# Latent products in high and low parts, latents split behind their norm, rotary keys copied behind the queries

## The chip, the core and the metric

The kernel runs on one core of one Trainium2 chip. TensorE (PE) does the matrix products, VectorE (DVE) and ScalarE (ACT) the work on whole tiles, GpSimd (POOL) one subtraction per weight slot and a few gathers, SyncE (SP) issues the weight transfers. The metric is the device time of one execution in microseconds (us), the median of several runs.

## What is computed

512 tokens of width 1024 pass through a first block (RG-LRU, sparse attention over latents, a routed mixture of experts) and then through two equal layers (neighbourhood, differential and latent attention, a gated feed-forward). All is in float32. The parts that the change touches are the products that read a normalised latent. In the first block:

```python
c_kv = rmsnorm(ckv, kv_norm_g)                       # (512, 256)
k = einsum('sr,rhd->shd', c_kv, w_uk)                # 8 heads of 128
v = einsum('sr,rhd->shd', c_kv, w_uv)
```

The reference folds `w_uk` into the queries and `w_uv` into the outputs; the kernel forms keys and values, which is the same sum. In each of the two layers:

```python
q  = rms_norm(c_q, q_norm_g) @ w_qb                  # 384 -> 8 heads of 64 + 32 rotary
kv = rms_norm(c_kv, kv_norm_g) @ w_kvb               # 256 -> 8 heads of 64 keys + 64 values
k  = concat([k_nope, broadcast(rope(k_rope))])       # one rotary key for all heads
o  = blocked_attention(q, k, v, 96 ** -0.5)
```

## The kernel before

Activations stand transposed, 128 features on the partitions and all 512 tokens in a row, so a product is one 128x128 weight chunk against 128x512 columns (for values the latent is the 128x128 side and the weight has the columns). The weights stream in slots of 16 chunks (1 MB) through a ring of five, `wring`. SP loads a slot when the one five places before is used up, and `w_used` counts slots that PE has left: it rises with PE's first matmul on the next slot.

There are two kinds of product. `tile` does one plain float32 matmul for each chunk, which the profile shows as two records. `tile3` does three matmuls in fp32r for each chunk: high weight by high operand, high weight by low operand, low weight by high operand (L459 to L461). For these, slots are split: `weights_hi` on ACT (L508) copies a slot into one of three `w_hi` buffers, and waits for `w_used` of the slot that held the buffer before; `weights_lo` on POOL (L518) then subtracts, and writes the low part over the ring's slot (`w_lo`, 128x2048). PE waits for `lo_rdy` of a split slot, and for the transfer alone of one that isn't split. Before the change the slots of uk and uv (28 and 29 of the first block) and of qb, kvb_k and kvb_v (29 to 31 of each layer) are not split.

The order of each engine is written out by hand; semaphores connect them. Around the change in a layer:

- **PE** runs the list `MIXED`: output tiles o0 to o7 of the differential attention, between them gate tiles ml_g0 to ml_g2, the squares of the latents (`squares_pe`, L470, behind `sq_added`) and the spreading of their norms (`spread_pe`, L479). For the second latent, ckv2, this reads o4, ml_g2, squares, o5, o6, spread, o7. Then come the rotary key's turn (L1120), the six query tiles of qb on `cq` with two turns between (L1056), four key tiles of kvb_k and four value tiles of kvb_v (L1137) on `ckv2`, and then the attention (L802), behind `roped` and `keys_rdy`. Tiles go to a small set of PSUM banks; from the third on, a tile needs the bank that ACT's copy of two tiles before has freed.
- **DVE** spreads the norm (L590), scales the latent in place (L1426, `lat_rdy`), merges output tiles (L1333, L1338), adds up squares (L564, L566), rotates the shared key (L1429 to L1432, `kr_rdy`), copies it to all heads (`k96`, L1435, `keys_rdy`), and rotates the queries in two groups (L1439, L1440, four additions L1444 each, `roped`).
- **ACT** applies the gates (L1183), copies the raw queries behind `kr_rdy` (`raw`, L1178), converts two slots (L508), copies queries (L1289, L1290), keys, and, behind `roped`, the values `vM` (L1178). In the attention it converts a further slot at units 4, 19 and 33 (`ml_weights`).
- **POOL** goes through the split slots in order.

In the first block uk and uv (L448, L2474) follow the queries, DVE scales `ckv` at L1984 long before, and the top-k selection runs on DVE beside them.

Of the kernel before, what the change touches and what calls it, by code (L numbers as in the profile page):

```python
# [8 lines left out]
P = 128  # L9
# [160 lines left out]
def build(nc, xT, wmod, wrest, wfirst, wlayers, consts, vectors, brow, frow, lamv, rpb, w13, w2, out):  # L170
# [2 lines left out]
    vcol, NVEC = vector_plan()  # L173
    n_slots1, n_slots2 = end1 // CHUNKS, size2 // CHUNKS

    unsplit = [("rg", "ckv"), ("uk", "att_out")]
    plain1 = {s for a, b in unsplit for s in range(one[a] // CHUNKS, one[b] // CHUNKS)} | {one["router"] // CHUNKS}
    plain2 = set(range(two["qb"] // CHUNKS, two["ml_g"] // CHUNKS))
    split = [s for s in range(n_slots1) if s not in plain1]
    split += [n_slots1 + l * n_slots2 + s for l in range(LAYERS) for s in range(n_slots2) if s not in plain2]  # L180
    order = {slot: q for q, slot in enumerate(split)}

    def split_no(slot):
# [3 lines left out]
    with ExitStack() as ctx:  # L187

        def at(name, kb, shape, dt=F32):
            return nc.alloc_sbuf_tensor_at(name, shape, dt, offset=(nc.sbuf_base + 2047) // 2048 * 2048 + int(kb * 1024))  # L190
# [251 lines left out]
        def tile(pe, bank, c0, rhs, nk, m=P, wait=None):  # L442

            for k in range(nk):
                w = chunk(pe, c0 + k)
                if wait is not None:
                    wait(k)
                ins = pe.matmul(bank, w[:, 0:m], rhs[:, k, :], start=(k == 0), stop=(k == nk - 1))  # L448
                if k < nk - 1:
                    said(ins)  # L450
            return ins

        def tile3(pe, bank, c0, hi, lo, nk, m=P, wait=None):

            for k in range(nk):
                wh, wl = chunk(pe, c0 + k)
                if wait is not None:
                    wait(k)
                said(pe.matmul(bank, wh[:, 0:m], hi[:, k, :], start=(k == 0), stop=False))  # L459
                pe.matmul(bank, wh[:, 0:m], lo[:, k, :], start=False, stop=False)  # L460
                ins = pe.matmul(bank, wl[:, 0:m], hi[:, k, :], start=False, stop=(k == nk - 1))  # L461
            return ins

        def squares_pe(pe, n):

# [129 lines left out]
            spread(dve)  # L595

        rstd = acc[:]

        def free_bank_b(dve):

# [411 lines left out]
        def layer_pe(pe, l):  # L1012
# [106 lines left out]
            pe.wait_ge(A.free, kr_copied)  # L1119
            pe.matmul(B.claim(pe)[0:MLA_QK, :], K("perm_m")[0:MLA_QK, 0:MLA_QK], krT[0:MLA_QK, :], start=True, stop=True).then_inc(B.full, 1)  # L1120

            pe.wait_ge(lat_rdy, (l + 1) * (MQC + KVC))
            turns = []
            for t in range(QB_TILES):
                tile(pe, A.claim(pe), base["qb"] + t * MQC, cq, MQC).then_inc(A.full, 1)
                if t < HEADS // 4:
                    turns.append(A.made)
                else:
                    n = t - HEADS // 4
                    if n < len(turns):  # L1130
                        turn(K("perm_m"), turns[n])
            for h in range(0, HEADS, 2):
                tile(pe, A.claim(pe), base["kvb_k"] + (h // 2) * KVC, ckv2, KVC).then_inc(A.full, 1)
            for s_ in range(NQB):
                b = A.claim(pe)
                for k in range(KVC):
                    ins = pe.matmul(b, ckv2[:, k, s_ * P:(s_ + 1) * P], chunk(pe, base["kvb_v"] + 4 * k, 4), start=(k == 0), stop=(k == KVC - 1))  # L1137
                    if k < KVC - 1:
                        said(ins)
                ins.then_inc(A.full, 1)  # L1140
# [35 lines left out]
        def layer_act(act, l):  # L1176
# [114 lines left out]
            for h in range(0, HEADS, 2):  # L1291
                two_heads(q96, h)
                if h == 0:
                    weights_hi(act, base["kvb_k"])
            act.wait_ge(merged_rdy, (3 * l + 2) * DC)
            for h in range(0, HEADS, 2):
                two_heads(k96, h)
# [27 lines left out]
        def layer_dve(dve, l):  # L1325
# [89 lines left out]
            for n, parts in enumerate(MIXED):  # L1415
                for kind, m in parts:
                    if kind == "o":
                        merge(1, m)
                if n in (1, 3):
                    sum_squares(dve, (MQC, KVC)[n // 2])  # L1420
                    inverse_root(dve, (MQ_RANK, KV_RANK)[n // 2], EPS)
                elif n in (2, 4):
                    X, c_n, g = ((cq, MQC, V(f"mq_g{l}")), (ckv2, KVC, V(f"mkv_g{l}")))[n // 4]
                    spread(dve)
                    for c in range(c_n):
                        STT(out=X[:, c, :], in0=X[:, c, :], scalar=g[:, c:c + 1], in1=rstd, op0=ALU.mult, op1=ALU.mult).then_inc(lat_rdy, 1)  # L1426
# [4 lines left out]
            dve.wait_ge(B.free, B.took)  # L1431
            TT(x, x, t, ALU.add).then_inc(kr_rdy, 1)  # L1432
            dve.wait_ge(kr_rdy, l + 1)

            dve.tensor_copy(k96[64:MLA_QK, :, :], krT[64:MLA_QK, :].unsqueeze(1).broadcast_to((32, HEADS, SEQ))).then_inc(keys_rdy, 1)  # L1435
            for g in range(HEADS // 4):
                x, t = raw[:, g, :], vM[:, g, :]
                dve.wait_ge(A.free, a + g + 1)
                step(TT(t, x, K("cos_m"), ALU.mult))  # L1439
                TT(x, B.take(dve), K("sin_m"), ALU.mult).then_inc(B.free, 1)  # L1440
                dve.wait_ge(B.free, B.took)
                for j in range(4):
# [233 lines left out]
        def _(act):  # L1676
# [184 lines left out]
        def _(dve):  # L1861
# [112 lines left out]
            for n in range(MOD_SLOTS):  # L1974
                dve.wait_ge(rest_mod_in[n % 2], 16 * (n // 2 + 1))
                for h in range(2):
                    ins = mod_tile(mods[:, n % 2, h * D:(h + 1) * D], MOD_FIRST + 2 * n + h)
                ins.then_inc(mod_used, 1)
                if n == 0:
                    inverse_root(dve, KV_RANK, EPS)  # L1980
                if n == 1:
                    spread(dve)
                    for c in range(KVC):
                        dve.scalar_tensor_tensor(out=ckv[:, c, :], in0=ckv[:, c, :], scalar=V("kv_g")[:, c:c + 1], in1=rstd,  # L1984
                                                 op0=ALU.mult, op1=ALU.mult).then_inc(ckv_rdy, 1)
                score_in(2 * n)
                score_in(2 * n + 1)
            dve.wait_ge(mod_used, 1 + MOD_SLOTS)
# [403 lines left out]
        def _(pe):  # L2392
# [71 lines left out]
                tile3(pe, A.claim(pe), one["q"] + m * DC, *u, DC).then_inc(A.full, 1)  # L2464
            pe.wait_ge(ckv_rdy, KVC)
            for m in range(HEADS):
                tile(pe, A.claim(pe), one["uk"] + m * KVC, ckv, KVC).then_inc(A.full, 1)
            for s in range(NQB):
                for n in range(2):
                    b = A.claim(pe)  # L2470
                    for k in range(KVC):

                        w = chunk(pe, one["uv"] + (2 * k + n) * 4, 4)
                        ins = pe.matmul(b, ckv[:, k, s * P:(s + 1) * P], w, start=(k == 0), stop=(k == KVC - 1))  # L2474
                        if k < KVC - 1:
                            said(ins)
                    ins.then_inc(A.full, 1)
            pe.wait_ge(gh_rdy, RC)
            rnn_bank = {}

# [467 lines left out]
```

## Time and profile before

| | us |
|---|---|
| median of 3 runs | 3163.84 |
| lowest, highest run | 3163.22, 3166.88 |
| span of the profiled execution | 3164.0 |
| PE busy | 3055.2 |
| DVE busy | 1653.4 |
| ACT busy | 992.4 |
| POOL busy | 974.6 |

The profiled execution's span, first to last instruction, is 3164.0 us, and its own time can be taken as that. In the profile, a busy PE is one with a matmul in its pipe; a record's length includes the pipe (0.39 us for a matmul that is followed by the next one after 0.23 us), so rates are read from starts. The timeline gives start, length, engine, line, output and inputs, a count for equal instructions in a row, and in brackets the idle time just before with what ended it. PEclk is the share of TensorE's full clock that was granted.

### The profile page before, as it was taken

Reading aid. Unit: us, or ns where it says so; the run is one execution under the profiler, and the core shown is the slowest. Engines: PE = TensorE matmul, PEld = TensorE weight load, DVE = VectorE, ACT = ScalarE, POOL = GpSimd, SP = SyncE. Lnnn points to the kernel's source line nnn. Section 1 sums busy time; section 2 is a strip of 40 time slices with the busy share of each in tenths; the row PEclk is TensorE's granted clock in tenths of the full one; section 3 lists DMA queues with packets and bytes.
Section 4 is the critical chain, followed back from the end, with each engine's and each line's share of the span. In section 5 each row is a group of like instructions: output and inputs, shape, how many; then the busy total and the mean of one; then the engine's idle time right before and its main releaser. Section 6 shows DMA issues by size and latency. Waiting matters only on the chain.

```text
span 3164.0 us, 34626 instructions
## 1 busy us (share of the span) xinstructions
PE 3055.2 (97%) x13776; PEld 2108.2 (67%) x13776; DVE 1653.4 (52%) x2794; ACT 992.4 (31%) x1415; POOL 974.6 (31%) x423
## 2 busy tenths in 40 slices
PE   7999999999999989999999999999999999999998
PEld 4777656743333367776656788887786765778886
DVE  5698956455554535574657422221757457732223
ACT  3653233200000144334343322223424444332212
POOL 3243103210000044332213544446442311444433
PEclk9999999999999999999999999999999999999999
DMA  6236212599999921211211222222121120222221
GB/s 258 95 112 247 107 54 85 208 384 427 427 427 427 414 79 67 79 68 54 93 41 67 80 93 94 106 94 90 64 81 66 67 93 14 92 81 93 94 94 53
DMA packets 64817, 448.44 MB, mean 142 GB/s; under 512 B 8526, under 2 KB 8814, under 8 KB 12448
## 3 DMA queue, kind: packets, MB, share of 16 engines
q1 hardware_dynamic: 60336, 436.25, 35.8%
q0 software_dynamic: 3760, 8.11, 0.8%
q8 instruction: 98, 1.61, 0.2%
q10 hardware_dynamic: 576, 2.10, 0.2%
q14 instruction: 47, 0.39, 0.0%
HBM read 445.93 MB, written 4.21 MB: 142 GB/s over the span
## 4 chain that ended last, share of the span: by engine, by line
PE 82%; DVE 8%; DMA 7%; ACT 2%; issue 1%; SPq 0%; DVEq 0%; ACTq 0%
PE ps L459 16%; PE ps L460 15%; PE ps L461 15%; DMA mring<-w 6%; PE ps L2576 3%; PE ps L802 2%; PE ps L781 2%; PE ps L2640 2%; PE ps L2488 2%; PE ps L448 2%; PE ps L783 2%; PE ps L782 2%; PE ps L972 2%; PE ps L1076 1%; PE ps L2577 1%
## 5 line engine op out<-in xcount | busy, mean ns | idle before, releaser
L518 POOL TENSOR_TENSOR w_lo<-wring,w_hi 128x2048 fp32r<-128x2048 f32 (+1 forms) x284 | 854.6, 3027 | 1636.5 <-ACT w_hi L508 1636.4
L459 PE MATMUL ps<-x_hi,w_hi 128*128 128x512 f32 (+1 forms) x1480 | 582.2, 393 | 8.5 <-ACT lru_t L1729 4.5
L461 PE MATMUL ps<-x_hi,w_lo 128*128 128x512 f32 (+1 forms) x1480 | 577.1, 390 | 0.0
L508 ACT ACTIVATE w_hi<-wring 128x2048 fp32r<-128x2048 f32 x176 | 335.9, 1911 | 317.8 <-PE ps L459 242.4
L460 PE MATMUL ps<-xf_lo,w_hi 128*128 128x512 f32 x1080 | 421.3, 390 | 0.0
L459 PEld LDWEIGHTS ps<-x_hi,w_hi 128*128 128x128 f32 (+1 forms) x1480 | 278.0, 188 | 77.7 <-ACT gb L1753 5.2
L461 PEld LDWEIGHTS ps<-x_hi,w_lo 128*128 128x128 f32 (+1 forms) x1480 | 278.1, 188 | 59.1
L2576 PE MATMUL ps<-mring,xT__96 128*64 128x512 f32 x512 | 238.2, 601 | 12.5 <-DMA mring<-w 7.2
L2577 PE MATMUL ps<-mring,xT__96 128*64 128x512 f32 x512 | 238.2, 601 | 0.0
L460 PEld LDWEIGHTS ps<-xf_lo,w_hi 128*128 128x128 f32 x1080 | 203.5, 188 | 41.2
L1457 DVE TENSOR_TENSOR g_f<-ps,g_f 128x512 f32<-128x512 f32 x44 | 30.4, 692 | 362.8 <-PE ps L461 350.0
L781 PE MATMUL ps<-x_hi,w_hi 128*128 128x512 f32 x336 | 162.3, 483 | 0.0
L460 PE MATMUL ps<-xa_lo,w_hi 128*128 128x512 f32 (+1 forms) x400 | 155.7, 389 | 0.0
L459 PE MATMUL ps<-g_hi,w_hi 128*128 128x512 f32 x352 | 137.7, 391 | 0.0
L461 PE MATMUL ps<-g_hi,w_lo 128*128 128x512 f32 x352 | 137.0, 389 | 0.0
L460 PE MATMUL ps<-g_lo,w_hi 128*128 128x512 f32 x352 | 137.0, 389 | 0.0
L1315 ACT ACTIVATE g_f<-ps 128x512 f32<-128x512 f32 x44 | 26.3, 598 | 351.4 <-PE ps L461 346.5
L1584 POOL DMA_INDIRECT xs<-u_rows,ids x15 | 15.4, 1029 | 391.4 <-PE ps L2563 365.1
L2576 PEld LDWEIGHTS ps<-mring,xT__96 128*64 128x64 f32 x512 | 65.1, 137 | 101.8 <-issue 82.3
L783 PE MATMUL ps<-x_hi,w_lo 128*128 128x512 f32 x336 | 132.1, 393 | 0.0
L782 PE MATMUL ps<-xa_lo,w_hi 128*128 128x512 f32 x336 | 131.9, 393 | 0.0
L2640 PE MATMUL ps<-mring,hidT 128*64 128x512 f32 x512 | 117.8, 597 | 2.6 <-DMA mring<-w 1.6
(567 smaller groups left out, 5563.5 us busy)
## 6 DMA issues: line engine op xcount, KB each, us to landing
mring<-w SPq DMA_DIRECT2D x192, 1024.0 KB, 23.2
wring<-wlayers SPq DMA_DIRECT2D x148, 1024.0 KB, 4.7
wring<-wfirst SPq DMA_DIRECT2D x44, 1024.0 KB, 4.8
mods<-wrest SPq DMA_DIRECT2D x16, 1024.0 KB, 4.8
wmodS<-wmod SPq DMA_DIRECT2D x3, 2048.0 KB, 17.6
rp<-rpb POOLq DMA_DIRECT2D x16, 192.0 KB, 2.7
hT<-xT SPq DMA_DIRECT2D x1, 2048.0 KB, 8.8
wmodS<-wmod SPq DMA_DIRECT2D x2, 1024.0 KB, 26.4
```

What stands on the lines that cost most here:

```text
L448: ins = pe.matmul(bank, w[:, 0:m], rhs[:, k, :], start=(k == 0), stop=(k == nk - 1))
L459: said(pe.matmul(bank, wh[:, 0:m], hi[:, k, :], start=(k == 0), stop=False))
L460: pe.matmul(bank, wh[:, 0:m], lo[:, k, :], start=False, stop=False)
L461: ins = pe.matmul(bank, wl[:, 0:m], hi[:, k, :], start=False, stop=(k == nk - 1))
L508: act.activation(w_hi[:, q % HI_SLOTS, :], wring[:, home(g), :], ACT.Copy).then_inc(hi_rdy, 1)
L518: ins = pool.tensor_tensor(w_lo[:, home(slot), o:o + n], wring[:, home(slot), o:o + n], w_hi[:, q % HI_SLOTS, o:o + n].bitcast(F32), ALU.s ...
L781: said(pe.matmul(state["bank"], wh, x[0][:, k, :], start=(k == 0), stop=False))
L782: pe.matmul(state["bank"], wh, x[1][:, k, :], start=False, stop=False)
L783: ins = pe.matmul(state["bank"], wl, x[0][:, k, :], start=False, stop=(k == DC - 1))
L2576: pe.matmul(ps[MOE_ROWS:P, 2 + a, :], x, w[:, 0:SEQ], start=(k == 0), stop=(k == DC - 1))
L2577: ins = pe.matmul(ps[0:MOE_ROWS, 2 + a, :], x, w[:, SEQ:D], start=(k == 0), stop=(k == DC - 1))
L2640: ins = pe.matmul(ps[n * MOE_ROWS:(n + 1) * MOE_ROWS, 5 + a, :], hidT[:, a, k, :], w[:, n * SEQ:(n + 1) * SEQ], start=(k == 0), stop=(k == 3))
```

## The change

The slots of uk, uv, qb, kvb_k and kvb_v are now split, and their products go through `tile3` (weights first) or the new `latent_values` (latent first). `latent_split` takes the place of the scaling in place: DVE writes the scaled latent to a scratch tile, casts it to a high part, and subtracts to get the low part, each step for all chunks before the next, with a wait between. PE waits for the first latent alone ahead of qb, and for the second ahead of kvb_k. The copy of the rotary key to all heads stands behind the rotation of the queries, since its place now holds scratch. ACT converts two more slots in the first block and three more in each layer, POOL subtracts as many.

```diff
-    unsplit = [("rg", "ckv"), ("uk", "att_out")]
+    unsplit = [("rg", "ckv"), ("rnn_out", "att_out")]
...
-    plain2 = set(range(two["qb"] // CHUNKS, two["ml_g"] // CHUNKS))
...
+        def latent_values(pe, s, at, hi):
+
+            b = A.claim(pe)
+            for k, c in enumerate(at):
+                wh, wl = chunk(pe, c, 4)
+                xh, xl = (x[:, k, s * P:(s + 1) * P] for x in (hi, ckv_lo))
+                said(pe.matmul(b, xh, wh, start=(k == 0), stop=False))
+                pe.matmul(b, xh, wl, start=False, stop=False)
+                ins = pe.matmul(b, xl, wh, start=False, stop=(k == KVC - 1))
+            ins.then_inc(A.full, 1)
...
+        def latent_split(dve, X, y, hi, lo, n, g, rdy):
+
+            for c in range(n):
+                ins = dve.scalar_tensor_tensor(out=y[:, c, :], in0=X[:, c, :], scalar=g[:, c:c + 1], in1=rstd, op0=ALU.mult, op1=ALU.mult)
+            after(dve, ins, dve_step, "dstep")
+            for c in range(n):
+                ins = dve.tensor_copy(hi[:, c, :], y[:, c, :])
+            after(dve, ins, dve_step, "dstep")
+            for c in range(n):
+                dve.tensor_tensor(lo[:, c, :], y[:, c, :], hi[:, c, :].bitcast(F32), ALU.subtract).then_inc(rdy, 1)
...
-            pe.wait_ge(lat_rdy, (l + 1) * (MQC + KVC))
+            pe.wait_ge(lat_rdy, l * (MQC + KVC) + MQC)
             turns = []
             for t in range(QB_TILES):
-                tile(pe, A.claim(pe), base["qb"] + t * MQC, cq, MQC).then_inc(A.full, 1)
+                tile3(pe, A.claim(pe), base["qb"] + t * MQC, cq_hi, cq_lo, MQC).then_inc(A.full, 1)
...
+            pe.wait_ge(lat_rdy, (l + 1) * (MQC + KVC))
             for h in range(0, HEADS, 2):
-                tile(pe, A.claim(pe), base["kvb_k"] + (h // 2) * KVC, ckv2, KVC).then_inc(A.full, 1)
+                tile3(pe, A.claim(pe), base["kvb_k"] + (h // 2) * KVC, ckv2_hi, ckv_lo, KVC).then_inc(A.full, 1)
             for s_ in range(NQB):
...
+                latent_values(pe, s_, [base["kvb_v"] + 4 * k for k in range(KVC)], ckv2_hi)
...
                 if h == 0:
-                    weights_hi(act, base["kvb_k"])
+                    weights_hi(act, base["kvb_k"], 1)
+            weights_hi(act, base["kvb_k"])
...
-            dve.tensor_copy(k96[64:MLA_QK, :, :], krT[64:MLA_QK, :].unsqueeze(1).broadcast_to((32, HEADS, SEQ))).then_inc(keys_rdy, 1)
             for g in range(HEADS // 4):
...
+            dve.wait_ge(A.free, a + QB_TILES)
+            dve.tensor_copy(k96[64:MLA_QK, :, :], krT[64:MLA_QK, :].unsqueeze(1).broadcast_to((32, HEADS, SEQ))).then_inc(keys_rdy, 1)
...
             for h in range(HEADS):
                 act.activation(kT[:, h, :], A.take(act), ACT.Copy).then_inc(A.free, 1)
+                if h == 0:
+                    weights_hi(act, one["uk"], 1)
```

`weights_hi` converts all split slots up to a few ahead of the one it is called for, so where slots become split, conversions move although the calls stay. The following lists give an engine's instructions in the order of the program; line numbers are those of the kernel listed.

DVE in layer 0, from the spread of the norm of cq to the sum of the squares of ckv2 (`acc`; `sqb` are squares from ACT), before:

```order
L590 COPY acc<-ps 128x512
L1426 SCALAR_TENSOR_TENSOR cq<-cq,vec,acc 128x512 x3
L1333 SCALAR_TENSOR_TENSOR df_gate<-df_gate,ps 128x512
L1338 TENSOR_TENSOR uT<-uT,df_gate 128x512
L564 COPY acc<-sqb 128x512
L566 TENSOR_TENSOR acc<-acc,sqb 128x512
```

and after:

```order
L603 COPY acc<-ps 128x512
L615 SCALAR_TENSOR_TENSOR cq_y<-cq,vec,acc 128x512 x3
L618 CAST cq_hi<-cq_y 128x512 x3
L621 TENSOR_TENSOR cq_lo<-cq_y,cq_hi 128x512 x3
L1354 SCALAR_TENSOR_TENSOR df_gate<-df_gate,ps 128x512
L1359 TENSOR_TENSOR uT<-uT,df_gate 128x512
L577 COPY acc<-sqb 128x512
L579 TENSOR_TENSOR acc<-acc,sqb 128x512
```

The three scalings write to scratch, and three casts and three subtractions stand between them and the merge of o4.

DVE in layer 0, from the rotation of the shared key `krT` to the first row of the attention, before:

```order
L1429 TENSOR_TENSOR raw<-ps,cs 32x512
L1430 TENSOR_TENSOR krT<-krT,cs 32x512
L1432 TENSOR_TENSOR krT<-krT,raw 32x512
L1435 COPY k_135<-krT 32x4096
L1439 TENSOR_TENSOR vM<-raw,cs 128x512
L1440 TENSOR_TENSOR raw<-ps,cs 128x512
L1444 TENSOR_TENSOR q_134<-vM,raw 32x512 x4
L1439 TENSOR_TENSOR vM<-raw,cs 128x512
L1440 TENSOR_TENSOR raw<-ps,cs 128x512
L1444 TENSOR_TENSOR q_134<-vM,raw 32x512 x4
L867 TENSOR_REDUCE small<-ps 128x1
```

and after:

```order
L1451 TENSOR_TENSOR raw<-ps,cs 32x512
L1452 TENSOR_TENSOR krT<-krT,cs 32x512
L1454 TENSOR_TENSOR krT<-krT,raw 32x512
L1459 TENSOR_TENSOR vM<-raw,cs 128x512
L1460 TENSOR_TENSOR raw<-ps,cs 128x512
L1464 TENSOR_TENSOR q_141<-vM,raw 32x512 x4
L1459 TENSOR_TENSOR vM<-raw,cs 128x512
L1460 TENSOR_TENSOR raw<-ps,cs 128x512
L1464 TENSOR_TENSOR q_141<-vM,raw 32x512 x4
L1466 COPY k_142<-krT 32x4096
L891 TENSOR_REDUCE small<-ps 128x1
```

The copy of the key (`k`) moved from ahead of the queries' rotation to behind it.

ACT in layer 0, from the squares of ckv2 to the first copies of keys, before:

```order
L494 ACTIVATE sqb<-ckv_131 128x512 x2
L1183 ACT_TABLE_LOAD
L1183 ACTIVATE sg_123<-ps,small 128x512
L553 ACT_TABLE_LOAD
L553 ACTIVATE small<-small 128x4
L1178 ACTIVATE raw<-ps 128x512 x2
L508 ACTIVATE w_hi<-wring 128x2048
L1289 ACTIVATE q_134<-ps 64x512
L1290 ACTIVATE q_134<-ps 64x512
```

and after:

```order
L507 ACTIVATE sqb<-ckv_131 128x512 x2
L521 ACTIVATE w_hi<-wring 128x2048
L1203 ACT_TABLE_LOAD
L1203 ACTIVATE sg_123<-ps,small 128x512
L566 ACT_TABLE_LOAD
L566 ACTIVATE small<-small 128x4
L1198 ACTIVATE raw<-ps 128x512 x2
L521 ACTIVATE w_hi<-wring 128x2048
L1309 ACTIVATE q_141<-ps 64x512
L1310 ACTIVATE q_141<-ps 64x512
```

One conversion now stands ahead of the gate ml_g2, and one more behind the copies of the queries, ahead of those of the keys. In the attention, the conversion at unit 4 is two in a row (L521 `w_hi<-wring 128x2048 x2`), where it was one.

## Rows read from the trace of the kernel before

**Rows 1.** the page, the chain that ended last, shares of the span by engine.

```profile
PE 82%; DVE 8%; DMA 7%; ACT 2%; issue 1%; SPq 0%; DVEq 0%; ACTq 0%
```

**Rows 2.** PE's timeline, layer 0: start, length (us), engine, line, operation, [idle, releaser].

```profile
1537.70 0.50 PE L459 MATMUL ps<-o_hi,w_hi 128*128 128x512 f32 x1
...
1546.00 0.95 PE L470 MATMUL ps<-cs,acc 128*128 128x1 f32 x8
...
1557.05 7.89 PE L448 MATMUL ps<-cq,wring 128*128 128x512 f32 x18
...
1581.09 7.03 PE L1137 MATMUL ps<-wring,ckv 128*128 128x512 f32 x16
1589.01 1.10 PE L802 MATMUL ps<-k,q 96*128 96x512 f32 x2 [0.89 <-ACT vM L1178]
...
1604.88 0.64 PE L972 MATMUL ps<-PT,cs 128*64 128x512 f32 x1 [1.19 <-ACT PT L917]
```

**Rows 3.** DVE's timeline, layer 0.

```profile
1539.01 2.08 DVE L1426 SCALAR_TENSOR_TENSOR cq<-cq,vec,acc 128x512 f32<-128x512 f32 x3
...
1542.78 0.69 DVE L566 TENSOR_TENSOR acc<-acc,sqb 128x512 f32<-128x512 f32 x1
...
1559.88 2.29 DVE L1435 COPY k<-krT 32x4096 f32<-32x4096 f32 x1
...
1566.63 9.67 DVE L1444 TENSOR_TENSOR q<-vM,raw 32x512 f32<-32x512 f32 x4
...
1577.78 2.83 DVE L1444 TENSOR_TENSOR q<-vM,raw 32x512 f32<-32x512 f32 x4
```

**Rows 4.** ACT's timeline, layer 0.

```profile
1546.20 0.69 ACT L1183 ACTIVATE sg<-ps,small 128x512 f32<-128x512 f32 x1 [11.08 <-PE ps L461]
...
1559.89 0.60 ACT L1178 ACTIVATE raw<-ps 128x512 f32<-128x512 f32 x1 [11.48 <-DVE krT L1432]
...
1562.90 1.90 ACT L508 ACTIVATE w_hi<-wring 128x2048 fp32r<-128x2048 f32 x1
```

**Rows 5.** PE's timeline, the first block's queries, keys and values.

```profile
365.69 0.39 PE L459 MATMUL ps<-x_hi,w_hi 128*128 128x512 f32 x1
...
366.37 0.39 PE L459 MATMUL ps<-x_hi,w_hi 128*128 128x512 f32 x1
...
373.85 13.89 PE L448 MATMUL ps<-ckv,wring 128*128 128x512 f32 x32
387.58 1.88 PE L2474 MATMUL ps<-wring,ckv 128*128 128x512 f32 x4
```

**Rows 6.** DVE's timeline, start of the first block's attention.

```profile
402.83 0.29 DVE L992 SCALAR_TENSOR_TENSOR Bb<-cs,sel 128x128 f32<-128x128 f32 x1 [11.22 <-PE ps L802]
```

**Rows 7.** DVE's timeline, layer 0: split, merge, later an FFN split.

```profile
1509.57 0.43 DVE L1353 CAST o_hi<-o 128x512 fp32r<-128x512 f32 x1
...
1510.63 0.42 DVE L1353 CAST o_hi<-o 128x512 fp32r<-128x512 f32 x1
...
1517.69 4.33 DVE L1338 TENSOR_TENSOR uT<-uT,df_gate 128x512 f32<-128x512 f32 x1
...
1797.53 1.13 DVE L1459 CAST g_hi<-g_f 128x512 fp32r<-128x512 f32 x1
```

**Rows 8.** POOL's timeline, layer 0, a few of its subtractions.

```profile
1516.86 4.61 POOL L518 TENSOR_TENSOR w_lo<-wring,w_hi 128x2048 fp32r<-128x2048 f32 x1 [7.54 <-ACT w_hi L508]
...
1564.88 9.45 POOL L518 TENSOR_TENSOR w_lo<-wring,w_hi 128x2048 fp32r<-128x2048 f32 x2 [30.84 <-ACT w_hi L508]
...
1793.77 4.60 POOL L518 TENSOR_TENSOR w_lo<-wring,w_hi 128x2048 fp32r<-128x2048 f32 x1 [1.50 <-ACT w_hi L508]
```

**Rows 9.** PE's timeline, first block, behind the longest early wait.

```profile
179.90 0.80 PE L459 MATMUL ps<-x_hi,w_hi 128*128 128x512 f32 x1 [4.10 <-ACT lru_t L1729]
```

**Rows 10.** windows there: stretch, busy by engine, PEclk, DMA share, GB/s.

```profile
180.00:182.00 2.00, 2.00 (x5) 1.63 (x6) 1.92 (x3) 0.33 (x1) 2.00 (x1) 0.50 0.27 41
182.00:184.00 2.00, 2.00 (x8) 1.59 (x8) 1.97 (x4) 1.21 (x2) 0.55 (x1) 0.82 0.81 307
```

More of the change, by code:

```diff
@@ L174, in build @@
     n_slots1, n_slots2 = end1 // CHUNKS, size2 // CHUNKS
-    unsplit = [("rg", "ckv"), ("uk", "att_out")]
+    unsplit = [("rg", "ckv"), ("rnn_out", "att_out")]
     plain1 = {s for a, b in unsplit for s in range(one[a] // CHUNKS, one[b] // CHUNKS)} | {one["router"] // CHUNKS}
-    plain2 = set(range(two["qb"] // CHUNKS, two["ml_g"] // CHUNKS))
     split = [s for s in range(n_slots1) if s not in plain1]
-    split += [n_slots1 + l * n_slots2 + s for l in range(LAYERS) for s in range(n_slots2) if s not in plain2]
+    split += [n_slots1 + l * n_slots2 + s for l in range(LAYERS) for s in range(n_slots2)]
     order = {slot: q for q, slot in enumerate(split)}
@@ L329, in build @@
         raw = at("raw", 149, [P, 2, SEQ])
+        cq_hi, cq_y, cq_lo = at("cq_hi", 137, [P, MQC, SEQ], F32R), at("cq_y", 112, [P, MQC, SEQ]), at("cq_lo", 112, [P, MQC, SEQ], F32R)
+        ckv_y, ckv_lo = at("ckv_y", 183, [P, KVC, SEQ]), at("ckv_lo", 183, [P, KVC, SEQ], F32R)
+        ckv_hi, ckv2_hi = at("ckv_hi", 179, [P, KVC, SEQ], F32R), at("ckv2_hi", 143, [P, KVC, SEQ], F32R)
         q96 = at("q96", 96, [P, HEADS, SEQ])
@@ L1131, in layer_pe @@
                         turn(K("perm_m"), turns[n])
+            pe.wait_ge(lat_rdy, (l + 1) * (MQC + KVC))
             for h in range(0, HEADS, 2):
-                tile(pe, A.claim(pe), base["kvb_k"] + (h // 2) * KVC, ckv2, KVC).then_inc(A.full, 1)
+                tile3(pe, A.claim(pe), base["kvb_k"] + (h // 2) * KVC, ckv2_hi, ckv_lo, KVC).then_inc(A.full, 1)
             for s_ in range(NQB):
[L1135 to L1140, printed above, removed]
+                latent_values(pe, s_, [base["kvb_v"] + 4 * k for k in range(KVC)], ckv2_hi)
             pe.wait_ge(roped, l * 16 + 16)
@@ L1422, in layer_dve @@
                 elif n in (2, 4):
-                    X, c_n, g = ((cq, MQC, V(f"mq_g{l}")), (ckv2, KVC, V(f"mkv_g{l}")))[n // 4]
                     spread(dve)
-                    for c in range(c_n):
-                        STT(out=X[:, c, :], in0=X[:, c, :], scalar=g[:, c:c + 1], in1=rstd, op0=ALU.mult, op1=ALU.mult).then_inc(lat_rdy, 1)
+                    if n == 2:
+                        latent_split(dve, cq, cq_y, cq_hi, cq_lo, MQC, V(f"mq_g{l}"), lat_rdy)
+                    else:
+                        latent_split(dve, ckv2, ckv_y, ckv2_hi, ckv_lo, KVC, V(f"mkv_g{l}"), lat_rdy)
             x = krT[64:MLA_QK, :]
@@ L1982, in _ @@
                     spread(dve)
-                    for c in range(KVC):
-                        dve.scalar_tensor_tensor(out=ckv[:, c, :], in0=ckv[:, c, :], scalar=V("kv_g")[:, c:c + 1], in1=rstd,
-                                                 op0=ALU.mult, op1=ALU.mult).then_inc(ckv_rdy, 1)
+                    latent_split(dve, ckv, ckv_y, ckv_hi, ckv_lo, KVC, V("kv_g"), ckv_rdy)
                 score_in(2 * n)
@@ L2466, in _ @@
             for m in range(HEADS):
-                tile(pe, A.claim(pe), one["uk"] + m * KVC, ckv, KVC).then_inc(A.full, 1)
+                tile3(pe, A.claim(pe), one["uk"] + m * KVC, ckv_hi, ckv_lo, KVC).then_inc(A.full, 1)
             for s in range(NQB):
                 for n in range(2):
[L2470 to L2477, printed above, removed]
+                    latent_values(pe, s, [one["uv"] + (2 * k + n) * 4 for k in range(KVC)], ckv_hi)
             pe.wait_ge(gh_rdy, RC)
```

## The prediction

> **What bounds the kernel now.** Read the page's chain first: TensorE holds 82% of the work that ended last, while DVE holds 8% and ScalarE 2% [rows 1]. So time that the change takes from PE's matmuls comes off the span, unless PE then waits, and time that it adds to DVE, ACT or POOL costs only where PE comes to wait for it. Next read PE's timeline of the latent part of a layer (layer 0; layer 1 shows the same rows). The squares of the second latent, the query tiles, the value tiles and the attention follow with one wait of 0.89 us, ahead of the attention [rows 2]. There is no slack on PE to absorb anything. Then read DVE's and ACT's timelines beside it, for how late each could be before PE notices [rows 3, 4]. Three margins decide the case:
> - DVE adds up the squares of ckv2 until 1543.47 (1542.78 + 0.69), and PE wants them at 1546.00: 2.5 us.
> - The rotated key (`kr_rdy`) is there just ahead of 1559.88, and ACT's first `raw` copy, which waits for it, is done at 1560.49. PE wants its bank for the third query tile at 1562.20 (six plain products, 5.15 us, behind 1557.05): 1.7 us.
> - The last query rope ends at 1580.61 (1577.78 + 2.83), and ACT's first copy of vM, 0.6 us like that of `raw`, waits for it. PE wants that bank for its third value tile, four products (3.43 us) behind 1581.09, at 1584.5: 3.3 us.
>
> **Products.** Three matmuls in parts go from 365.69 to 366.37, 0.68 us; 16 plain products go from 373.85 to 387.58, 0.858 us each [rows 5]. So a product gets 0.178 us cheaper. The first block has 32 of them (uk, uv): 5.7 us. A layer has 34 (qb 18, kvb_k 8, kvb_v 8): 6.05 us. Were that all, the time would be 3164.0 - 17.8 = 3146.2 us.
>
> **First block.** Two weight conversions on ACT, two on POOL and 2 casts and 2 subtractions on DVE are added. DVE waits 11.22 us for PE at the start of the attention [rows 6], so with PE 5.7 us earlier 5.5 us of that are left, and the products' gain is kept. The DVE additions (2.1 us, below) and a blocked operation (4.6 us) add up to 6.7 us, so at worst 1.2 us more than is left; I take nothing.
>
> **A layer, the split of the latents.** A cast of 128x512 takes 0.43 us and the pair of cast and subtraction comes every 1.06 us (1509.57 to 1510.63) [rows 7]. Behind the norm of cq that is 3 pairs, 3.2 us, and behind that of ckv2 2 pairs, 2.1 us, both in front of what DVE did next: the merge of o4 and the squares of ckv2; the merge of o7 and the rotary key.
>
> **A layer, POOL's new subtractions.** Each `w_lo` of 128x2048 takes some 4.6 us on POOL [rows 8]. A DVE operation that reads two SBUF tiles doesn't run beside it: the merge at 1517.69, 0.69 us elsewhere, took 4.33 us and ended as the `w_lo` of 1516.86 did; the cast at 1797.53 took 1.13 us instead of 0.43 [rows 7, 8] until a `w_lo` that ran from 1793.77 to 1798.37 was done. The four rope additions of 1566.63 took 9.67 us instead of 2.83 beside two `w_lo` in a row [rows 3, 8]. The Trainium skill, page "SBUF — State Buffer", section "Who interferes with whom", states this as a rule: a port pair shared by DVE and GpSimd is an exclusive lock, held for the whole instruction, and issue order decides who blocks. By that rule the other order is possible too, in which the casts go first and POOL waits, which is the second case below; the rows above agree with the lock.
>
> The new `w_lo` of slot 29 (qb) is where it matters. ACT may convert the slot when PE's first matmul of o4 is done, 1537.70 + 0.50 [rows 2]. It starts there, in an idle stretch of 11.08 us that ends at 1546.20, and needs 1.90 us [rows 4], so POOL takes the port at 1540.2 to 1540.5. DVE is then in the three scalings of 1539.01 (2.08 us) [rows 3], and its new casts come right behind. They, or the last scaling, wait some 4.5 us. The squares of ckv2 are late by 3.2 + 4.5 = 7.7 us; less the margin of 2.5 us **PE waits 5.1 us** (7.7 - 2.5, less 0.1 for the replay named below). Without the collision it would be 0.7 us; these are the bounds.
>
> **A layer, what follows.** Relative to PE, I carry the three margins on.
> - Third query tile: the key is 2.1 us later (the ckv2 split), and two tiles before it take 6 x 0.178 = 1.05 us less: 1.7 - 2.1 - 1.05 leaves **1.4 us of waiting**. Bounds: 0 to 1.4, and to 6 us if another `w_lo` fell there; none is due.
> - Third kvb_k tile: it needs the bank of ACT's first copy of k, and a third `w_hi`, 1.90 us [rows 4], now stands in front of that copy. ACT follows PE tile by tile there, so nearly all of it shows: **1.7 us**, by the replay named next, between 0 and 1.9.
> - Third kvb_v tile: the ropes end later by the 5.1 us of PE's wait, 2.1 us of the split and a third `w_lo` of 4.5 us beside them, less the 2.29 us of the k96 copy [rows 3], which now stands behind: 9.4 us. PE itself is later by 5.1 + 1.4 + 1.7 less 30 products' 5.3 us: 2.9 us. With the margin of 3.3 us PE waits 3.2 us; replayed, operation by operation, from the durations of these rows it is 4.2 us, because a `w_lo` shifts as well when DVE holds the port. I take the middle, **3.7 us**, and 0 is the other bound: without the third block (4.5 us) the wait is gone.
> - The k96 copy itself is covered: behind the ropes PE still has two kvb_v tiles (2.7 us) and a copy before the attention.
> - Attention unit 4: ACT converts two slots instead of one there. PE's wait for the turned P, 1.19 us [rows 2], which stands behind the first conversion, grows by **1.9 us**; bounds 0.7 (if ACT's own idle takes 1.2) and 1.9.
>
> Sum of a layer: 5.1 + 1.4 + 1.7 + 3.7 + 1.9 - 6.05 = +7.75 us. Two layers and the first block: 15.5 - 5.7 = +9.8 us.
>
> **The clock.** After a wait of PE of 4.10 us at 179.90 the granted clock stood at 0.50 (1.2 GHz) for 2 us and 0.82 in the next 2 us [rows 9, 10]: 1.0 + 0.36 = 1.36 us lost. The wait of 5.1 us is longer than that one, so I count it there, once a layer: 2.7 us. The 3.7 us wait is shorter than the one shown: 0 or 2.7 us more, and I take 0. That gives **3164.0 + 9.8 + 2.7 = 3176.5 us**. The span is 0.2 us from the median of the runs, so nothing is added.
>
> **Rivals.**
> - *Forecast*: all five new waits, 3173.8 (no clock loss) to 3179.2 (at both waits), with 2 us of slips either way: 3172 to 3181. For: each wait is worked out from a row, and the collision needs no coincidence finer than 2 us, since casts and subtractions fill 1541 to 1544.5 and POOL starts inside. 0.55.
> - *DVE keeps the port, faster*: the place is the `w_lo` of slot 29 and those beside the ropes. If POOL has to wait until DVE's row of operations has a gap, or starts only after the squares are added (1543.47 + 3.2 = 1546.7, some 6 us later than I worked out), PE waits 0.7 us at the squares and not at all for the ropes. A layer then stands at 0.7 + 1.4 + 1.7 + 1.9 - 6.05 = -0.35 us, the whole at 3164.0 - 0.7 - 5.7 = 3157.6; with the other three waits at their lower bounds (0, 0, 0.7) at -4.65 us a layer and 3149.0. Against it: in the rows above it was DVE that waited, and ACT, idle since 1535, has nothing that holds the conversion back. 0.23, of which 0.18 is beyond the bound below.
> - *Half blocked*: the squares wait but the ropes don't: 5.1 + 1.4 + 1.7 + 1.9 - 6.05 = +4.05 a layer, so 3166.4, with clock loss 3169. It holds if DVE gets between the second and the third `w_lo`. 0.14.
> - *More*: clock loss at every wait, the 3 us of unit 4 among them, and a port wait in the first block: 3179.2 + 2.7 + 1.2 = 3183, and up to 3188 with one more `w_lo` in front of a key. 0.06.
> - *The products aren't cheaper* would need matmuls of the latent's parts to run slower than 0.227 us; their tiles and types are those of [rows 5], so it gets 0.02, at 3176.5 + 17.8 = 3194.
>
> **The numbers.** 0.2% (6.3 us) is about what a measurement of this kernel tells from no change. Faster: 0.18. Same: 0.05 + 0.14 = 0.19. Slower: 0.55 + 0.06 + 0.02 = 0.63. The range from 3153 to 3184 leaves out half of the second case, most of "more" and the last, and the forecast's slips, about 0.2 in all. The forecast's own range is 3172 to 3181.
>
> **What the profile of the changed kernel would show.** Right: a cast behind the norm of cq of 4 to 5 us with a `w_lo` beside it; PE waiting about 5 us at the squares of ckv2 with DVE's sum as releaser, and a clock near 0.5 behind it; 3 to 4 us ahead of the third kvb_v tile, for ACT's vM behind the ropes; 3 us in unit 4; an attention that starts some 6 to 9 us later in layer 0 than the first block's lead of 5.7 us would have it. Wrong: casts of 0.4 us and a wait of under 1 us at the squares (the port), or rope additions of 2.8 us (the third `w_lo`). If the first block's attention doesn't come 5 us earlier, my price of a product or its slack is wrong.

## The result and the profile after

The changed kernel takes 3184.52 us in the median (3184.01 to 3186.95) where the kernel before, on the same chip in the same hour, took 3165.36 us. The ratio is 1.006, with a 95% interval from 1.0048 to 1.0071: slower by some 19 us. The forecast was slower, 3176.5 us, with a range up to 3184.0. So the direction was right, the size was not, and the time lies just above the range. In the two traces, which the account below goes by, the span grew from 3164.0 to 3182.1 us.

The page of the changed kernel: span, busy times, and the chain that ended last (answers [rows 1]).

```profile
span 3182.1 us, 34878 instructions
PE 3049.8 (96%) x13876; PEld 2130.0 (67%) x13876; DVE 1681.1 (53%) x2818; ACT 1006.9 (32%) x1423; POOL 1011.7 (32%) x431
PE 79%; DVE 10%; DMA 7%; ACT 2%; issue 2%; SPq 0%; POOL 0%; DVEq 0%; ACTq 0%
```

PE is busy for 5.4 us less and the span is 18.1 us longer, so PE is idle for 23.5 us more; DVE's share of the chain rose from 8% to 10%. PE's timeline of layer 0 shows where (start, length, operation, idle before and releaser; compare [rows 2], where only the last two waits stood):

```profile
1545.99 1.86 PE L483 MATMUL ps<-cs,acc 128*128 128x1 f32 x8 [4.79 <-DVE acc L579]
...
1565.37 0.50 PE L461 MATMUL ps<-cq_hi,w_hi 128*128 128x512 f32 x1 [0.91 <-ACT raw L1198]
...
1579.96 0.50 PE L461 MATMUL ps<-ckv_hi,w_hi 128*128 128x512 f32 x1 [1.37 <-ACT k L1310]
...
1588.57 0.50 PE L472 MATMUL ps<-w_hi,ckv_hi 128*128 128x512 f32 x1 [2.61 <-ACT vM L1198]
1593.68 1.10 PE L826 MATMUL ps<-k,q 96*128 96x512 f32 x2 [0.89 <-ACT vM L1198]
...
1611.35 1.11 PE L996 MATMUL ps<-PT,cs 128*64 128x512 f32 x1 [2.99 <-ACT PT L941]
```

All five waits of the forecast are there, in the places that were named: four are new, and that of unit 4 grew from 1.19 us. DVE's and POOL's timelines show the first one's origin (compare [rows 3, 8]):

```profile
1534.06 6.43 DVE L615 SCALAR_TENSOR_TENSOR cq_y<-cq,vec,acc 128x512 f32<-128x512 f32 x3
1540.52 1.10 DVE L618 CAST cq_hi<-cq_y 128x512 fp32r<-128x512 f32 x3
1541.65 1.90 DVE L621 TENSOR_TENSOR cq_lo<-cq_y,cq_hi 128x512 fp32r<-128x512 f32 x3
...
1569.40 9.88 DVE L1464 TENSOR_TENSOR q<-vM,raw 32x512 f32<-32x512 f32 x4
1579.31 4.98 DVE L1459 TENSOR_TENSOR vM<-raw,cs 128x512 f32<-128x512 f32 x1
```

```profile
1535.35 4.60 POOL L531 TENSOR_TENSOR w_lo<-wring,w_hi 128x2048 fp32r<-128x2048 f32 x1 [6.26 <-ACT w_hi L521]
...
1567.69 9.61 POOL L531 TENSOR_TENSOR w_lo<-wring,w_hi 128x2048 fp32r<-128x2048 f32 x2 [27.75 <-ACT w_hi L521]
1578.77 4.97 POOL L531 TENSOR_TENSOR w_lo<-wring,w_hi 128x2048 fp32r<-128x2048 f32 x1 [1.46 <-ACT w_hi L521]
```

The three scalings of cq took 6.43 us instead of 2.08: the `w_lo` of slot 29 fell into them, and it was the last scaling that waited, not the casts. That scaling by itself:

```profile
1535.39 5.10 DVE L615 SCALAR_TENSOR_TENSOR cq_y<-cq,vec,acc 128x512 f32<-128x512 f32 x1
```

The third `w_lo` beside the ropes fell on the scaling of the second group of raw queries, which took 4.98 us.

Then the windows of PE's clock (stretch; busy time of PE, PEld, DVE, ACT, POOL; PEclk; DMA share; GB/s):

```profile
1546.00:1552.00 6.00, 6.00 (x18) 5.13 (x19) 1.00 (x6) 0.21 (x1) 0.00 (x0) 0.50 0.00 0
1552.00:1554.00 2.00, 2.00 (x9) 1.55 (x9) 0.98 (x2) 0.00 (x0) 0.00 (x0) 0.87 0.00 0
1590.00:1592.00 2.00, 2.00 (x6) 1.57 (x6) 0.20 (x1) 0.60 (x1) 0.00 (x0) 0.52 0.00 0
1592.00:1594.00 2.00, 1.11 (x3) 0.36 (x3) 0.00 (x0) 1.16 (x2) 0.00 (x0) 0.63 0.00 0
1612.00:1616.00 4.00, 4.00 (x12) 1.16 (x10) 0.00 (x0) 0.00 (x0) 4.00 (x2) 0.50 0.02 4
1616.00:1618.00 2.00, 2.00 (x7) 0.32 (x3) 0.00 (x0) 0.00 (x0) 1.50 (x1) 0.65 0.00 0
```

Behind three of the waits PE ran at half clock (0.50 is the lower of its two levels, 1.2 GHz), each time for longer than in [rows 10]. A table of PE's starts in both traces gives the account. The last column is how much further the changed kernel fell behind since the row above.

| PE at | before | after | behind by | change |
|---|---|---|---|---|
| first block's first uk product | 373.85 | 373.65 | -0.20 | |
| first block's attention | 402.25 | 396.35 | -5.90 | -5.70 |
| layer 0, squares of cq | 1530.37 | 1525.41 | -4.96 | +0.94 |
| layer 0, squares of ckv2 | 1546.00 | 1545.99 | -0.01 | +4.95 |
| layer 0, key's turn | 1556.19 | 1559.33 | +3.14 | +3.15 |
| layer 0, attention | 1589.01 | 1593.68 | +4.67 | +1.53 |
| layer 0, unit 4's P by values | 1604.88 | 1611.35 | +6.47 | +1.80 |
| layer 0, next scores | 1608.46 | 1617.91 | +9.45 | +2.98 |
| layer 1, squares of cq | 2539.71 | 2547.13 | +7.42 | -2.03 |
| layer 1, squares of ckv2 | 2555.34 | 2567.70 | +12.36 | +4.94 |
| layer 1, key's turn | 2565.52 | 2580.51 | +14.99 | +2.63 |
| layer 1, attention | 2598.34 | 2615.23 | +16.89 | +1.90 |
| layer 1, next scores behind unit 4 | 2617.79 | 2636.50 | +18.71 | +1.82 |
| last hidden product | 3142.31 | 3161.28 | +18.97 | +0.26 |

### The profile page after: what moved, and what is told of

Same layout as the page of the kernel before. It is cut to its first block, busy times and chain, and to the rows that moved or that the text cites. A ratio compares the mean times of both kernels' runs of the same rounds, so it can differ in the third digit from the quotient of the medians.

```text
span 3182.1 us, 34878 instructions
## 1 busy us (share of the span) xinstructions
PE 3049.8 (96%) x13876; PEld 2130.0 (67%) x13876; DVE 1681.1 (53%) x2818; ACT 1006.9 (32%) x1423; POOL 1011.7 (32%) x431
## 4 chain that ended last, share of the span: by engine, by line
PE 79%; DVE 10%; DMA 7%; ACT 2%; issue 2%; SPq 0%; POOL 0%; DVEq 0%; ACTq 0%
PE ps L461 16%; PE ps L463 15%; PE ps L462 15%; DMA mring<-w 6%; PE ps L2591 3%; PE ps L826 3%; PE ps L805 2%; PE ps L2655 2%; PE ps L807 2%; PE ps L806 2%; PE ps L2503 2%; PE ps L996 2%; PE ps L843 1%; PE ps L2592 1%; PE ps L1100 1%
## 5 line engine op out<-in xcount | busy, mean ns | idle before, releaser
L531 POOL TENSOR_TENSOR w_lo<-wring,w_hi 128x512 fp32r<-128x512 f32 (+1 forms) x292 | 891.6, 3071 | 1621.6 <-ACT w_hi L521 1621.5
L521 ACT ACTIVATE w_hi<-wring 128x2048 fp32r<-128x2048 f32 x184 | 351.0, 1912 | 325.5 <-PE ps L461 250.9
```

Source lines behind the costliest of these rows:

```text
L521: act.activation(w_hi[:, q % HI_SLOTS, :], wring[:, home(g), :], ACT.Copy).then_inc(hi_rdy, 1)
L531: ins = pool.tensor_tensor(w_lo[:, home(slot), o:o + n], wring[:, home(slot), o:o + n], w_hi[:, q % HI_SLOTS, o:o + n].bitcast(F32), ALU.s ...
```

## The experiments

The theory after the result: POOL's `w_lo` of slot 29 holds the port that DVE needs, which makes PE wait; the clock that falls behind the wait is a cost of its own, and larger than forecast; the third `w_lo` and the conversions on ACT make the rest. The rivals: DVE's own extra operations make the waits; the slow matmuls have another reason; the first block's gain is lost. "Behind by" below is always from PE's starts, as in the table.

**e1, the first block alone.** The change's first-block part is kept, the layers stand as before.

```diff
-    split += [n_slots1 + l * n_slots2 + s for l in range(LAYERS) for s in range(n_slots2)]
+    plain2 = set(range(two["qb"] // CHUNKS, two["ml_g"] // CHUNKS))
+    split += [n_slots1 + l * n_slots2 + s for l in range(LAYERS) for s in range(n_slots2) if s not in plain2]
...
```

> Only uk and uv of the first block are split; the layers stand as before. Theory (the first block gains, the layers lose): the sparse attention starts 5.9 us earlier as in the changed kernel and most of it lasts to the end: 5 to 6 us faster than before, a span of 3158 to 3159 us. Rival (the gain of the first block is lost in the transfer-bound expert stage, where the changed kernel's lead fell from 5.9 to 5.0 us): the lead is gone at the first expert product or at the layers, within 2 us of before.

Measured: 0.9987 of before (0.9977 to 0.9997), some 4 us faster where 5 to 6 us were expected, span 3160.0 us. From the first uk product to the attention PE needs 22.7 us instead of 28.4, here as in every kernel with this part: 5.7 us, as worked out. The lead at the attention was 3.72 us in this trace and 5.90 in that of the changed kernel, because the start differs from run to run: the first uk product came at 375.83 us here, at 373.65 in the changed kernel and at 373.85 before. From the attention to layer 0 a further 0.60 us of the lead went (0.95 in the changed kernel). That stretch, which the change leaves alone, was between 1.25 us shorter (e4) and 3.79 us longer (e6) than before in the traces below. So the gain is real and mostly kept, and a few microseconds of any single span are spread of the stages ahead of the layers; what an experiment does is read from its own stretch.

**e2, POOL behind the squares.** The changed kernel with one wait more.

```diff
+                    if slot == two["qb"] // CHUNKS:
+                        pool.wait_ge(sq_added, 23 + 5 * l)
```

> The changed kernel, with POOL waiting for the sum of the squares of ckv2 before the w_lo of slot 29. Theory (port collision plus half clock behind PE's wait): DVE's scalings take 2.1 us instead of 6.43, PE's wait at the squares falls from 4.79 to about 0.7 us, the granted clock stays at 1.00 behind it (it cost 3.15 us), so 7.2 us a layer less: a span near 3168 us, against 3182. Rival (DVE's own six extra operations make the wait): PE still waits 3 us or more there, gain under 4 us in all.

Measured: 1.002 of before (1.001 to 1.0029), where the changed kernel has 1.006: some 12 us less. The ten runs spread from 3166.79 to 3175.6 us, and the profiled one, with a span of 3166.3 us, is among the shortest. DVE's timeline, the same operations as above, and the one that now meets the `w_lo`; then PE's, and windows behind the squares and around the value tiles:

```profile
1534.02 2.08 DVE L615 SCALAR_TENSOR_TENSOR cq_y<-cq,vec,acc 128x512 f32<-128x512 f32 x3
...
1543.44 2.78 DVE L597 TENSOR_TENSOR small<-small 128x4 f32<-128x4 f32 x1 [0.30 <-ACT small L566]
```

```profile
1541.60 1.05 PE L483 MATMUL ps<-cs,acc 128*128 128x1 f32 x8 [0.43 <-DVE acc L579]
```

```profile
1546.00:1552.00 6.00, 6.00 (x31) 5.03 (x30) 5.65 (x12) 0.00 (x0) 0.21 (x1) 1.00 0.51 175
1574.00:1586.00 12.00, 8.50 (x34) 5.79 (x33) 8.52 (x7) 5.91 (x9) 2.26 (x1) 1.00 0.24 87
```

The wait at the squares is 0.43 us, and the clock stays at 1.00. From the squares of cq to the key's turn a layer now loses 0.66 and 0.69 us instead of 8.10 and 7.57. DVE's six extra operations are still there, so the meeting with the `w_lo` made the wait, and they make at most the 0.43 us that are left. The `w_lo` now meets a small operation, 2.78 us instead of 0.16, for which nobody waits.

**e3, filler in front of the wait.** Nothing is earlier, but PE does five idle matmuls into the bank that it has claimed, in place of waiting empty.

```diff
+            b = B.claim(pe) if fill else None
+            for _ in range(fill):
+                pe.matmul(b, ident, K("cos_d"), start=True, stop=True)
             pe.wait_ge(sq_added, cnt["sq_p"])
...
```

> The changed kernel, with five idle matmuls (4.3 us) on PE in front of the wait for the squares of ckv2; nothing is earlier. Theory (the clock's loss is a cost of its own, caused by the empty wait): PE's wait becomes about 0.5 us, the clock stays at 1.00, squares to spread takes 6.4 us instead of 9.5, so 3.1 us a layer: 6 us less, a span near 3176 us. Rival (the matmuls behind the wait are slow for another reason, such as late weights): no change, 3182 us, or slower if the fillers delay the squares.

Measured: 1.005 of before (1.0034 to 1.0067), span 3179.3 us. PE's timeline and the window behind:

```profile
1542.29 4.45 PE L482 MATMUL ps<-cs 128*128 128x512 f32 x10
1547.23 1.05 PE L486 MATMUL ps<-cs,acc 128*128 128x1 f32 x8 [0.49 <-DVE acc L582]
```

```profile
1547.00:1553.00 6.00, 5.77 (x29) 4.95 (x30) 2.56 (x9) 0.21 (x1) 0.00 (x0) 1.00 0.12 23
```

Squares to key's turn cost +0.07 and +0.11 us over before, where the changed kernel had +3.15 and +2.63. So the clock behind this one wait is worth 5.6 us in the two layers, apart from the wait itself. The whole time can't show it (the intervals of this kernel and the changed one overlap), and the span shows 2.8 us of it: this run's lead at the first block's attention was 1.6 us smaller than the changed kernel's, and unit 4 of layer 1 lost 1.7 us more here.

**e4, one conversion at unit 4.**

```diff
-                    weights_hi(act, base["ml_g"] + (4, 19, 33).index(i) * CHUNKS)
+                    weights_hi(act, base["ml_g"] + (4, 19, 33).index(i) * CHUNKS, 1 if i == 4 else 2)
```

> The changed kernel, with one weight conversion at attention unit 4 and the other put off to unit 19. Theory (the second conversion stands in front of the turned P, and the longer wait takes the clock with it in layer 0): PE's wait falls from 2.99 to 1.2 us in both layers, and the 2.98 us of clock in layer 0 go too: 1.8 + 1.8 + 3.0 = 6.6 us less, a span near 3175.5 us. Rival (the second conversion costs the same at unit 19): no change, 3182 us.

Measured: 1.0064 of before (1.0047 to 1.008): no gain. Unit 4 did what was expected: PE's wait is 1.19 us again, and attention to next scores costs +0.03 us in both layers instead of +4.78 and +1.82. But between there and the attention's end 2.6 us came back in either layer. ACT's timeline at unit 19, and PE's:

```profile
1651.32 3.71 ACT L521 ACTIVATE w_hi<-wring 128x2048 fp32r<-128x2048 f32 x2
```

```profile
1655.66 1.13 PE L826 MATMUL ps<-k,q 96*128 96x512 f32 x2 [1.99 <-ACT P L930]
```

Two conversions in a row cost about as much there. The rival was right in substance: a conversion that is put off isn't a conversion that is hidden. The 1.4 us that remained are less than the start's spread (the first uk product came 3.7 us later here than in the changed kernel).

**e6, POOL behind the ropes.** On top of e2, POOL waits for the last rope before the third `w_lo`.

```diff
+                    if slot == two["ml_g"] // CHUNKS:
+                        pool.wait_ge(roped, l * 16 + 16)
```

> POOL behind the squares, and POOL waiting for the last rope before w_lo of slot 32; the third conversion stays ahead of the key copies. Theory: the 2.61 us wait ahead of the third value tile goes (the scaling of the second rope group, 4.98 us in the changed kernel, is 0.7 us again), the 1.37 us wait of the key tile stays. Rival: the key tile's wait is what keeps PE, and the value tile's wait grows into its place: no gain of the stretch.

Measured: a single run, with a span of 3164.5 us; its starts are what counts. The scaling of the second group of raw queries takes 0.69 us again, the wait of the value tile is gone, and that of the key tile stays:

```profile
1576.49 0.69 DVE L1459 TENSOR_TENSOR vM<-raw,cs 128x512 f32<-128x512 f32 x1
...
1577.12 0.50 PE L461 MATMUL ps<-ckv_hi,w_hi 128*128 128x512 f32 x1 [1.35 <-ACT k L1310]
```

Key's turn to attention takes 2.59 and 2.57 us less than before; with POOL behind the squares alone it took 0.31 and 1.89 us more. The theory holds.

**e5, and the third conversion behind the keys.** On top of e6, the call that converts slot 32 moves behind the copies of the keys.

```diff
-            weights_hi(act, base["kvb_k"])
             act.wait_ge(merged_rdy, (3 * l + 2) * DC)
             for h in range(0, HEADS, 2):
                 two_heads(k96, h)
+            weights_hi(act, base["kvb_k"])
```

> The kernel with POOL behind the squares, and two more moves: ACT's third conversion stands behind the copies of the keys instead of ahead of them, and POOL waits for the last query rope before the w_lo of that slot (32). Theory (the waits ahead of the third key tile, 1.37 us, and the third value tile, 2.61 us, come from these two): both go, the stretch from the key's turn to the attention takes 5 to 6 us less than before instead of 0.3 to 1.9 us more, since the clock holds as well; 8 to 12 us less than with POOL behind the squares alone: a span of 3155 to 3158 us. Rival (the ropes are late because of the first two w_lo and the split of ckv2): the vM wait stays above 1.5 us, gain under 4 us.

Measured: 0.9999 of before (0.9989 to 1.0008), span 3162.4 us. Smaller than expected: 3.00 us less than before in either layer, against 5 to 6. The key tile's wait went, and 0.77 us of it came back ahead of the third value tile:

```profile
1577.95 0.50 PE L472 MATMUL ps<-w_hi,ckv_hi 128*128 128x512 f32 x1 [0.77 <-ACT vM L1198]
```

**e8, conversions in quarters.** The changed kernel, with the attention's conversions of slots 33 to 35 cut into four of 512 columns, one in each of units 4 to 7, 9 to 12 and 19 to 22.

```diff
...
-                if i in (4, 19, 33):
-                    weights_hi(act, base["ml_g"] + (4, 19, 33).index(i) * CHUNKS)
+                for first in (4, 9, 19):
+                    if first <= i < first + 4:
+                        weights_hi_piece(act, i - first)
+                if i == 33:
+                    weights_hi(act, base["ml_g"] + 2 * CHUNKS)
```

(`weights_hi_piece` converts one piece and counts the slot as converted with its last.)

> The changed kernel, with the conversions of the attention in quarters, and nothing else. Theory (a whole conversion of 1.9 us in front of a turned P costs PE about 1.2 us wherever it stands, a second one 1.8 us more, and the longer wait can cost 3 us of clock): the wait of 2.99 us at unit 4 and the one that came back at unit 19 go: 9 us less than the changed kernel, a span of 3172 to 3175 us. Rival (four short ones delay four units): gain under 3 us.

Measured: 1.0043 of before (1.0027 to 1.0058), span 3175.3 us. A quarter takes 0.64 us, PE waits for nothing at unit 4, and attention to next scores takes 1.23 us less than before in both layers, where the changed kernel took 4.78 and 1.82 us more: 9.1 us, as expected. The span is 6.8 us shorter; from the first block's attention to layer 0 this run lost 2.0 us more than the changed kernel.

```profile
1607.51 0.64 ACT L531 ACTIVATE w_hi<-wring 128x512 fp32r<-128x512 f32 x1
1609.08 0.66 ACT L531 ACTIVATE w_hi<-wring 128x512 fp32r<-128x512 f32 x1
```

**e7, all together.** e5 and e8, and the casts and subtractions of ckv2 stand behind the rotation of the key.

```diff
-                        latent_split(dve, ckv2, ckv_y, ckv2_hi, ckv_lo, KVC, V(f"mkv_g{l}"), lat_rdy)
+                        latent_scaled(dve, ckv2, ckv_y, KVC, V(f"mkv_g{l}"))
...
             dve.wait_ge(kr_rdy, l + 1)
+            latent_parts(dve, ckv_y, ckv2_hi, ckv_lo, KVC, lat_rdy)
...
```

> All together: POOL behind the squares and behind the ropes, the third conversion behind the key copies, casts and subtractions of ckv2 behind the rotation of the key, and the conversions of the attention in quarters of 512 columns at units 4 to 7, 9 to 12 and 19 to 22. Theory: the wait for raw (0.91 us) goes too, and no unit waits for a conversion: each layer is 5.5 to 9 us shorter than before, the whole 3145 to 3152 us, faster than before by 0.4 to 0.6%. Rival (ACT or DVE becomes the bound of the stretch, or the quarters cost their own start-up in every unit): not under 3158 us.

Measured: 0.9972 of before (0.9962 to 0.9982), median 3156.12 us, span 3151.8 us: faster than both kernels, and than the one before by 0.28%, where 0.4 to 0.6% was expected. From the key's turn to the attention of layer 0 PE waits in these two places only:

```profile
1578.58 0.50 PE L472 MATMUL ps<-w_hi,ckv_hi 128*128 128x512 f32 x1 [0.76 <-ACT vM L1215]
1582.53 1.10 PE L843 MATMUL ps<-k,q 96*128 96x512 f32 x2 [0.92 <-ACT vM L1215]
```

That stretch takes 4.17 us less than before in both layers. The products' 6.05 us less the new wait would be 5.3; a further 1.1 us sits in gaps of 0.05 to 0.1 us at the starts of tiles, which no single row explains. Just behind the attention's start PE now waits for POOL, which was held back for the ropes:

```profile
1584.30 0.47 PE L822 MATMUL ps<-x_hi,w_hi 128*128 128x512 f32 x1 [0.67 <-POOL w_lo L543]
```

So from the squares of cq to the scores behind unit 4 a layer is 3.8 us shorter than before, not 5.5 to 9, and the first block's lead had shrunk to 2.99 us by layer 0 in this run.

## Why the size was wrong, point by point

- **Products, first block.** 5.7 us forecast, 5.70 measured, in every trace. DVE's 11.22 us of slack [rows 6] became 5.50. Right.
- **Port collision at the scalings.** Forecast a PE wait of 5.1 us, measured 4.79 and 4.78. Right, and e2 shows that it is the collision: moving POOL alone removes all but 0.43 us. The Trainium skill, page "SBUF — State Buffer", section "Who interferes with whom", says that the port pair which DVE and GpSimd share is an exclusive lock, and that issue order decides who blocks. The trace agrees: the `w_lo` started at 1535.35 and the third scaling at 1535.39, and it was the scaling that took 5.10 us instead of 0.75.
- **raw, key tile, value tile, unit 4.** Forecast 1.4, 1.7, 3.7 and 1.9 us, measured 0.91, 1.37, 2.61 and 1.80. The places and causes were right, the sizes together 2.0 us a layer too large. e5 and e6 show the causes of the key and value tile, e4 and e8 that of unit 4, and e7, where the wait for raw is gone with the casts behind the key's rotation, that of raw.
- **The clock: the term that failed.** The forecast took 1.36 us from [rows 9, 10], once a layer, 2.7 us in all. The squares' wait alone cost 3.15 us in layer 0 and 2.63 in layer 1 (e3 gives them back): the clock stood at 0.50 for 6 us, not 2. The value tile's wait, for which the forecast took 0 because it is shorter than the 4.10 us of the yardstick, cost clock as well: with the same waits at full clock (e2, layer 0) the key's turn to the attention takes 0.32 us more than before, in the changed kernel 1.53 and 1.90, so 1.2 and 1.6 us. Unit 4's cost 2.98 us in layer 0 and nothing in layer 1. With e3's 5.6 us for the squares that is 5.6 + 2.8 + 3.0 = 11.4 us instead of 2.7. Only the rival "more" counted a loss at every wait, at the yardstick's price, and it got 0.06.
- **The sum.** Forecast +12.5, measured +18.1 in the traces. Clock +8.7 over the forecast; the waits, with the squares' 0.3 us, -2.3 us a layer, together -4.6; the lead at layer 0 4.96 us instead of 5.7, +0.7. The kernel before lost 2.0 us at the end of layer 0 that the changed one didn't (the account's row for layer 1): its clock fell there and the other's didn't. The rest, 2.8 us, is about the gaps at the starts of tiles: in layer 0 of e2 the three waits of 4.88 us less the products' 6.05 should have gained 1.17 us, and 0.32 were lost, so 1.5 us a layer. The forecast had no such term. With clock and gaps the attention of layer 0 starts 10.4 us later than the lead of 5.7 us would have it, where 6 to 9 were expected. The page of the profile says the same from another side. PE's 23.5 us of added idle time are the five waits, 11.5 us a layer. Its busy time fell by 5.4 us instead of the products' 17.8, and the 12.4 us between are the clock's 11.4, less the 2.0 lost before, and 3.0 of gaps.
- **Span for time.** The forecast added nothing because the span was 0.2 us from the median of the runs. But a run's time is 1.8 us or more longer than its own span in every run here (3184.13 and 3182.1 us for the profiled run of the changed kernel). So 3176.5 us was a span, and the time that belongs to it is about 3178.3.
- **Luck.** The waits that were made too long hid 4.6 us of the clock's error, and the kernel before's own 2.0 us another part. That the time lies only 0.5 us above the range is no sign that the sum was nearly right.

What stays open: why the clock fell for longer or shorter, or not at all, behind equal waits of 2.99 us at unit 4, and why the value tile's 2.61 us cost clock in layer 0 of the changed kernel and not in layer 0 of e2.

## What to carry to other kernels

A work item that is added to a side engine (here POOL's subtraction) is charged where it starts: before adding it, look what the engine that shares its port does at that moment, and if that is on the way to PE's next wait, let the side engine wait for a point in the other's work where it idles, and check that PE doesn't then wait for the side engine, as it did for 0.67 us in e7. A wait on PE costs its length and then the clock behind it; price the second from several rows, since it was as large as the wait in places here. Here long conversions in front of a step that PE waits for were hidden by cutting them and spreading the pieces over steps, not by putting them off. And a span is compared with a span, a time with a time.

## What the runs showed of the hardware

Two waits of equal length, 2.99 us, in the same place of two equal layers, differed by 3 us in what followed: behind the first the clock was 0.50 for 4 us and 0.65 for 2 more, behind the second it stayed at 1.00.

```profile
2632.92 0.64 PE L996 MATMUL ps<-PT,cs 128*64 128x512 f32 x1 [2.99 <-ACT PT L941]
2632.00:2636.00 4.00, 3.08 (x16) 1.05 (x16) 0.00 (x0) 1.44 (x3) 4.00 (x2) 1.00 0.00 0
```

The other kernels with two conversions at unit 4 (e2, e3, e5, e6) have the same wait of 2.98 or 2.99 us in both layers: behind six of these eight waits 1.70 us were lost, behind two nothing. In layer 0 of e2:

```profile
1602.00:1608.00 6.00, 5.32 (x17) 1.50 (x17) 0.00 (x0) 1.21 (x3) 6.00 (x2) 0.72 0.00 0
```

So the clock's loss is a risk behind a wait rather than a fixed price. It also means that small shifts change the time elsewhere: the kernel before fell to 0.50 around a wait of 0.81 us in the layer norm of layer 0, where the changed kernel, with the same work and the same wait, stayed at 1.00. Before, and the changed kernel's window of the same wait as the last line:

```profile
1767.39 2.08 PE L628 MATMUL ps<-cs,small 128*128 128x128 f32 x8 [0.81 <-DVE small L587]
...
1766.00:1768.00 2.00, 1.20 (x5) 0.61 (x4) 1.53 (x7) 0.21 (x1) 0.00 (x0) 0.63 0.00 0
1768.00:1770.00 2.00, 2.00 (x8) 1.59 (x8) 0.50 (x1) 0.00 (x0) 0.00 (x0) 0.50 0.00 0
1770.00:1772.00 2.00, 2.00 (x4) 0.85 (x3) 2.00 (x4) 1.12 (x2) 0.00 (x0) 0.50 0.00 0
...
1776.00:1778.00 2.00, 1.20 (x9) 1.19 (x10) 1.25 (x5) 0.00 (x0) 0.00 (x0) 1.00 0.00 0
```
